# Ups and downs with the moving operand read from the last column to the first

## What is computed

```
q = (h @ w_query)                        # 8 heads x 2 halves x 128
s1, s2 = scores of q against 128 keys each;  top 16 of each, top 16 of the 256 sums
expert_idx (T, 8, 16),  gates = softmax(top_s)
a = gelu(u[expert_idx] . h)              # u: 16384 experts x 1024
y = sum over the chosen experts of gates * a * v[expert_idx]
```

## Time and profile before

| | us |
|---|---|
| runs | 1440.38, 8263.65, 1440.93 |
| median | 1440.93 |
| the profiled execution | 1441.41 |
| its span | 1439.4 |

### The profile page before, as it was taken

One profiled execution on the slowest core, in us unless ns is written; L12 is line 12 of the kernel. 1 busy time (PEld: TensorE's weight loads), 2 busy tenths in 40 slices (PEclk: granted clock), 3 DMA queues, 4 the chain that ended last, 5 costly groups with the idle time before them and its releaser, 6 DMA issues.

```text
span 1439.4 us, 20447 instructions
## 1 busy us (share of the span) xinstructions
PE 1431.6 (99%) x7551; PEld 1277.2 (89%) x7551; DVE 1133.4 (79%) x1876; ACT 574.4 (40%) x799; POOL 979.8 (68%) x533
## 2 busy tenths in 40 slices
PE   9999999999999999999999999999999999999998
PEld 7766798899999999999999999888888888888887
DVE  6678551769999999699999995498777777777775
ACT  5775453333333333444444444333333333333332
POOL 3421544346888788866766675599887888878883
PEclk9999999999999999999999999999999999999999
DMA  6221332235778888989999986998888888888883
GB/s 227 103 89 45 103 113 100 89 100 184 251 262 268 273 272 273 348 281 364 355 360 355 372 296 230 371 383 340 346 346 346 327 326 345 344 341 328 331 302 117
DMA packets 122293, 381.57 MB, mean 265 GB/s; under 512 B 11768, under 2 KB 28280, under 8 KB 122240
## 3 DMA queue, kind: packets, MB, share of 16 engines
q1 hardware_dynamic: 70384, 202.69, 39.5%
q0 software_dynamic: 36864, 134.23, 25.3%
q10 hardware_dynamic: 14992, 44.06, 7.8%
HBM read 336.89 MB, written 44.06 MB: 265 GB/s over the span
## 4 chain that ended last, share of the span: by engine, by line
PE 95%; DVE 2%; DMA 1%; ACT 1%; issue 0%; SPq 0%; DVEq 0%
PE bank L748 28%; PE bank L749 28%; PE bank L750 28%; PE bank L1004 6%; PE bank L936 1%; DMA wf<-a_dram 1%; PE bank L884 1%; PE bank L907 0%; PE wide L896 0%; DVE pad L1235 0%; PE bank L815 0%; PE wide L815 0%; PE bank L826 0%; PE bank L822 0%; PE wide L822 0%
## 5 line engine op out<-in xcount | busy, mean ns | idle before, releaser
L484 POOL TENSOR_TENSOR wl<-raw,wh 128x1024 fp32r<-128x1024 f32 x208 | 507.7, 2442 | 277.7 <-ACT wh L514 275.1
L748 PE MATMUL bank<-hh,wh 128*128 128x384 f32 (+1 forms) x1184 | 416.2, 352 | 0.2 <-DVE hl L1251 0.2
L749 PE MATMUL bank<-hl,wh 128*128 128x384 f32 (+1 forms) x1184 | 406.4, 343 | 0.0
L750 PE MATMUL bank<-hh,wl 128*128 128x384 f32 (+1 forms) x1184 | 406.4, 343 | 0.0
L748 PE MATMUL bank<-wh,Wh 128*128 128x512 f32 x768 | 299.0, 389 | 0.7 <-DVE Wl L1458 0.7
L750 PE MATMUL bank<-wh,Wl 128*128 128x512 f32 x768 | 298.8, 389 | 0.0
L749 PE MATMUL bank<-wl,Wh 128*128 128x512 f32 x768 | 298.8, 389 | 0.0
L514 ACT ACTIVATE wh<-raw 128x1024 fp32r<-128x1024 f32 (+1 forms) x217 | 227.8, 1050 | 141.4 <-PE bank L750 136.4
L748 PEld LDWEIGHTS bank<-hh,wh 128*128 128x128 f32 x1184 | 222.8, 188 | 7.9 <-DVE hl L1251 0.6
L749 PEld LDWEIGHTS bank<-hl,wh 128*128 128x128 f32 x1184 | 222.8, 188 | 7.1 <-issue 0.2
L750 PEld LDWEIGHTS bank<-hh,wl 128*128 128x128 f32 x1184 | 222.3, 188 | 7.6
(11 more groups left out here) (200 smaller groups left out, 1628.6 us busy)
## 6 DMA issues: line engine op xcount, KB each, us to landing
raw<-uT_dram SPq DMA_DIRECT2D x128, 512.0 KB
xraw<-v_dram SPq DMA_DIRECT2D x72, 512.0 KB, 8.5
raw<-v_dram SPq DMA_DIRECT2D x56, 512.0 KB, 9.1
a_dram<-act_a ACTq DMA_DIRECT2D x64, 384.0 KB
wf<-a_dram SPq DMA_DIRECT2D x32, 768.0 KB, 6.8
raw<-wst_dram SPq DMA_DIRECT2D x40, 512.0 KB
gates_dram<-gbuf ACTq DMA_DIRECT2D x32, 512.0 KB
gt<-gates_dram SPq DMA_DIRECT2D x32, 512.0 KB, 4.0
```

What stands on the lines that cost most here:

```text
L484: pool.tensor_tensor(wl[:, n % SPLIT, :], raw_of(n), wh[:, n % SPLIT, :].bitcast(F32), ALU.subtract).then_inc(w_lo, 1)
L748: pe.matmul(dst, ah, bh, start=start, stop=False)
L749: pe.matmul(dst, ah, bl, start=False, stop=False)
L750: return pe.matmul(dst, al, bh, start=False, stop=stop)
```

## The change

In the ups and the downs the moving operand is passed with its columns reversed (`[:, ::-1]`), so that the first column that enters is the last in memory. The output pattern in PSUM stays as it was, so the banks hold the columns in mirrored order. What reads those banks reads them backwards: the gelu of an up, and the six last copies. The residual transposes of the three dense frame blocks write backwards and at mirrored places, so that x lies under the mirrored sums; those of the first block, which the dense downs do not touch, stay forward. The number of instructions, their order on each engine, their waits, the tiles and the transfers are the same in both kernels; the four early ups, the queries, the attention half and the gates stay as they were.

```diff
--- before.py
+++ after.py
@@ -680,7 +680,7 @@
                 if j % 2 == 0:
                     act.wait_ge(a_out[(j // 2) % 2], 16 * (j // 4))
                 act.wait_ge(w_used, n + 1)
-                act.activation(a_of(j), bank[n % 2][:, 0:DT], ACT.Gelu).then_inc(out_done, 1)
+                act.activation(a_of(j), bank[n % 2][:, 0:DT][:, ::-1], ACT.Gelu).then_inc(out_done, 1)
                 hi_to(n + SPLIT)
                 if j % 2:
                     act.wait_ge(out_done, done_up(j))
@@ -738,24 +738,29 @@
 
             for b in range(DB):
                 act.wait_ge(y_done, 2 * b + 2)
-                act.activation(y[:, (1 + b) * D + T:(2 + b) * D], bank[2 * b + 1][:, :], ACT.Copy).then_inc(act_copied, 1)
+                act.activation(y[:, (1 + b) * D + T:(2 + b) * D], bank[2 * b + 1][:, ::-1], ACT.Copy).then_inc(act_copied, 1)
 
 
         @block.tensor
         def _(pe):
+            def backwards(columns):
+
+                return columns[:, ::-1]
+
             def three(dst, ah, al, bh, bl, start, stop):
 
                 pe.matmul(dst, ah, bh, start=start, stop=False)
                 pe.matmul(dst, ah, bl, start=False, stop=False)
                 return pe.matmul(dst, al, bh, start=False, stop=stop)
 
-            def project(dst, s, right_h, right_l, between=None, order=range(KD), at=slice(0, T), first=0, last=KD - 1):
+            def project(dst, s, right_h, right_l, between=None, order=range(KD), at=slice(0, T), first=0, last=KD - 1,
+                        side=lambda columns: columns):
 
                 for k in order:
                     if between is not None:
                         between(k)
                     done = three(dst, wh[:, s, k * P:(k + 1) * P], wl[:, s, k * P:(k + 1) * P],
-                                 right_h[:, k, at], right_l[:, k, at], k == first, k == last)
+                                 side(right_h[:, k, at]), side(right_l[:, k, at]), k == first, k == last)
                 if order[-1] == last:
                     done.then_inc(w_used, 1)
 
@@ -959,7 +964,7 @@
 
                 pe.wait_ge(w_lo, n + 1)
                 pe.wait_ge(out_done, n - (QUERY_W + 1))
-                project(bank[static % 2][:, 0:DT], static % SPLIT, hh, hl, between, at=slice(FIRST, T))
+                project(bank[static % 2][:, 0:DT], static % SPLIT, hh, hl, between, at=slice(FIRST, T), side=backwards)
 
             def ups_of(first, count):
 
@@ -1014,7 +1019,9 @@
 
                 for half in range(2):
                     for kk in range(4):
-                        last = pe.matmul(bank[done + half][:, kk * P:(kk + 1) * P], x[:, 4 * half + kk, b * P:(b + 1) * P],
+                        to = (bank[done + half][:, kk * P:(kk + 1) * P] if b == 0 else
+                              backwards(bank[done + half][:, T - (kk + 1) * P:T - kk * P]))
+                        last = pe.matmul(to, x[:, 4 * half + kk, b * P:(b + 1) * P],
                                          ident, start=(kk == 0), stop=(b == 0 and kk == 3), is_transpose=True)
                 return last
 
@@ -1041,7 +1048,8 @@
                         for half in range(2):
                             at, d = slice(b * P, (b + 1) * P), slice(half * T, (half + 1) * T)
                             done = three(bank[2 * b + half][:, :], Wh[s][:, c, at], Wl[s][:, c, at],
-                                         wh[:, static % SPLIT, d], wl[:, static % SPLIT, d], False, end)
+                                         backwards(wh[:, static % SPLIT, d]), backwards(wl[:, static % SPLIT, d]),
+                                         False, end)
                             if end:
                                 done.then_inc(y_done, 1)
                     if not end:
@@ -1482,7 +1490,7 @@
             dve.tensor_copy(y[:, 0:D], wide[:, :]).then_inc(dve_copied, 1)
             for b in range(DB):
                 dve.wait_ge(y_done, 2 * b + 1)
-                dve.tensor_copy(y[:, (1 + b) * D:(1 + b) * D + T], bank[2 * b][:, :]).then_inc(dve_copied, 1)
+                dve.tensor_copy(y[:, (1 + b) * D:(1 + b) * D + T], bank[2 * b][:, ::-1]).then_inc(dve_copied, 1)
 
 
 _OUT = "out_dram"
```

## The result

The changed kernel takes 1469.16 us (median of 4, 1468.90 to 1469.38) against 1440.80 us before: the ratio is 1.0198 with a 95% interval of 1.0178 to 1.0218, so 28.4 us slower. The loss is clear of the noise; whether it is a little under or over 2% is not settled. One of the four runs of the kernel before took 8263.65 us, for a reason that nothing on record shows; without it the median would be 1440.67. The forecast was 1441 us in a range of 1427 to 1458. The profiled execution took 1469.38 us for a span of 1467.4.

The account below looks back on a forecast made before the run. The prediction took TensorE's matmuls, by the distance between starts, to bound the kernel. All terms were taken at 0, so the sum was 0 and the forecast 1441 us, in a range of 1427 to 1458.

Parts of the forecast that it names:

- What bounds the kernel: Whole kernel: TensorE is busy 1431.6 of 1439.4 us, so time is number of matmuls by distance between two starts.
- Gelu, split, residual, last copies at 0: PSUM accesses beside ups and downs: backward costs 0; upper bounds 2.6 us for residual, 0.6 us for last copies.
- Columns. I take 0: Ups and downs: a reversed column keeps its price of 0.418 ns, adding 0; upper bound 970.7 us.
- Starts. I take 0: Ups and downs: the fixed 12.7 ns of every matmul stays, adding 0; range a fifth either way, 13.4 us.
- ScalarE's jumping PSUM read: Gate copy, jumping 128 columns after every element: 599 ns for 512, plain copy 598; taken as nearest row on direction.
- dearer-start rival: Every up and down matmul: the fixed part of 12.7 ns doubles, 67.1 us more, 1508 us; chance 4%.
- half-rate rival: Every up and down: a descending operand comes at one fetch a column, 970.7 us more, 2412 us; chance 10%.
- Its last line: Ups and downs: the prediction's closing test, that a change of 5.5 ns per matmul is enough to make it wrong.
- cheaper start rival: Ups and downs: mirrored order avoids 8.0 ns of each matmul's fixed start, 42 us less, 1399 us; chance 7%.
- gate record: Float32 gate matmul of 128 columns, 111.7 ns: read as 4.7 ns beyond twice its columns.

Follow-up runs that it names:

- the readers alone: Changed kernel with all moving operands forward again; gelu, last copies and residual transposes still backward: 1440.45 us against 1440.67 for the kernel before, ratio 0.9999.

## Why the prediction was wrong

- **What bounds the kernel** was right: the time is matmuls by the distance of two starts, and the result comes out of that product within 1 us.
- **Gelu, split, residual, last copies at 0** were right, shown by the readers alone. The residual was where the Trainium skill was weighed (PSUM — Partial Sum Buffer, Specifications (TRN2)): 16 backward transposes take 1.74 us, where the doubling that the prediction took as the bound for that rule would give some 3.5, so a descending unit step isn't one of its slow patterns.
- **"Columns. I take 0", with "Starts. I take 0" beside it, is the step that failed**: the distance between two starts was put down as the same in either direction, and it grew by 4.6 ns at 384 columns and by 6.6 at 512. The zero took ScalarE's jumping PSUM read as the nearest row and called a descending address milder. That row is of another engine and another memory, at 1.17 ns an element where TensorE takes 0.417, and it bounds nothing here: a jump in the moving operand, every second column, costs 340.9 ns for 384, twice the price. That figure also goes against the rule of the Trainium skill given with the rival (SBUF — State Buffer, Specifications (TRN2), at least two hits on a 16-byte line for full bandwidth): two columns to a line don't suffice for this operand, while the 16-byte group itself is borne out by the aligned and shifted fours.
- **How the loss divides between columns and starts** the runs don't settle. The range for the starts, a fifth either way or 2.5 ns, had no row behind it. From 448 to 512 columns backward distances grow by 0.417 ns a column, no more than forward ones from 384 to 512, with 20.0 ns beyond the columns where forward has 13.3 at 512: by that reading it is the start that grew, the dearer-start rival at about half its size. At 384 17.8 ns lie beyond the columns, and at 320 nothing is lost, so over the whole range a dearer column with a cheaper start describes it about as well. A sum of one price a column and one a start, the form in which the prediction reckoned, doesn't hold for this operand.
- **The half-rate rival** had the right place and sign, but its size was 34 times too large (970.7 us against 28.4). Its last line was met all but exactly: a change of 5.5 ns a matmul was to be enough, and 5.4 were measured. Between a fifth of the start (13.4 us) and a whole one (67.1 us, the dearer-start rival) the range was empty, and that is the error in the range: 5.4 ns a matmul moved the time past its top by 11 us.
- **The cheaper start rival** rested on a misread row. It took the 111.7 ns of a gate record as a start of 4.7 ns on top of columns; backward float32r matmuls of 64, 128 and 192 columns settle at the same 111.7 ns, so it reads better as a floor that doesn't depend on the columns. Whether it is the floor of the weight load that each of them carries, no run here separates.

What stays open: why order between the groups costs what it does. Runs of 8, 16, 24, 32, 48, 64 and 96 in descending order cost 180, 177, 177, 176, 181, 173.5 and 176 ns, which no count of steps explains, and blocks of 16 cost 200. That the distances repeat with a period, keep a phase, need several starts to settle, change with the weight columns loaded beside them and, for an ascending read, with its place speaks for two streams, moving reads and weight loads, that meet in turn; that is argued and not shown. A matmul without a weight load beside it was not tried.

## What to carry to other kernels

On an engine that is busy 99% of the span, an access pattern that looks neutral has to be bounded from both sides at that engine's own rate, and the range has to cover the few nanoseconds per instruction that, times 5280, decide. In a kernel like this one, keep TensorE's float32r moving operand ascending, beginning on 16 bytes (by itself not a guarantee: 2 to 3 ns more at some places); a mirror, if one is needed, cost nothing in blocks of 128 columns here, nor in runs of 64 in an up of 384, nor on the side that reads PSUM. Several forms in the slots of one loop can be told apart in a single trace, if the first starts of each are left out.

## What was not expected of the hardware

- Order inside an aligned group of four float32 is free to TensorE's moving read (173 ns for 384); the same order shifted by one or two columns costs 256.5 ns, +48%.
- Every second column of the moving operand costs 340.9 ns for 384, every fourth 347.0, where adjacent columns cost 173.3.
- Fewer adjacent weight columns make a forward matmul of 512 dearer: 226.7 ns with 128, 230.0 with 64, 231.7 with 32.
- Backward float32r matmuls of 64, 128 and 192 columns, each with its weight load, all settle at 111.7 ns.
- A reversed moving operand costs 6.7 ns a matmul at 512 columns, 4.5 at 384, nothing at 320, and at 256 it is some 1.5 ns cheaper (118.3 against 119.8).
- An ascending read of 384 columns costs 173.3 or 175.6 ns by where it begins, both on a group of four.
